# Joint decode in another order: three sparse key tiles of half 0 moved behind the forget-gate exponentials and between the first values

## What is computed

```python
def fox_attend(q, qpos, cq, segs):
    logits = concat([einsum('bthd,bshd->bhts', q, k) * ATTN_SCALE + cq_t - ck_t for k, _, _, ck in segs])
    pr = masked_softmax(logits, mask)          # exp(logits - max) / sum, over all past and new keys
    out = sum(einsum('bhts,bshd->bthd', pr_seg, v) for each segment)

def nsa_cmp_sel(q, qpos, ck_raw, cv_raw, sk, sv, p):
    ...                                         # compressed scores choose 16 blocks of 64 rows
    lg = einsum('bqgrd,bgqksd->bgrqks', q_c, kg) * ATTN_SCALE - slope * dist
    o = einsum('bgrqn,bgqnd->bqgrd', masked_softmax(lg, mask), vg)

def sample_layer(x, cache, page_table, p):
    o_cmp, o_sel = nsa_cmp_sel(qa, qpos, cat(c_cmp_k, ck), cat(c_cmp_v, cv), cat(c_sel_k, sk), cat(c_sel_v, sv), p)
    o_win = window_attend(...)
    o_fox = fox_attend(fq, qpos, c_new, ((past k, v), (new k, v)))
    h = merge_branches(x, o_cmp, o_sel, o_win, ng, o_fox, ga, gb, p)
```

## Time and profile before

| | us |
|---|---|
| median of 3 runs | 931.16 |
| lowest, highest | 929.49, 931.47 |
| the profiled execution's own time | 930.13 |
| its span | 927.4 |

### The profile page before, as it was taken

One profiled execution on the slowest core, in us unless ns is written; L12 is line 12 of the kernel. 1 busy time (PEld: TensorE's weight loads), 2 busy tenths in 40 slices (PEclk: granted clock), 3 DMA queues, 4 the chain that ended last, 5 costly groups with the idle time before them and its releaser, 6 DMA issues. The chain is left out here.

```text
span 927.4 us, 18075 instructions
## 1 busy us (share of the span) xinstructions
PE 859.7 (93%) x7225; PEld 704.6 (76%) x7225; DVE 518.3 (56%) x949; ACT 374.0 (40%) x694; POOL 160.6 (17%) x262
## 2 busy tenths in 40 slices
PE   2999888799999999999999977999979999999996
PEld 1888768689889977655755456997678988989884
DVE  5466568533434667654467434656665655656555
ACT  3346575642424323453224412445144434444330
POOL 1200041311121122333434510000010100101000
PEclk9999989999999999999999989999979999999999
DMA  5543096175424379989999994975064444554412
GB/s 168 189 158 119 5 313 240 64 160 144 153 93 183 102 314 371 335 312 421 415 416 418 379 404 140 289 244 171 1 225 138 137 136 157 198 188 136 136 45 61
DMA packets 90609, 191.89 MB, mean 207 GB/s; under 512 B 7434, under 2 KB 68651, under 8 KB 78155
## 3 DMA queue, kind: packets, MB, share of 16 engines
q0 software_dynamic: 15408, 106.04, 29.6%
q1 hardware_dynamic: 73836, 84.43, 29.4%
q10 hardware_dynamic: 1296, 0.45, 0.2%
HBM read 187.44 MB, written 7.64 MB: 210 GB/s over the span
## 5 line engine op out<-in xcount | busy, mean ns | idle before, releaser
L1604 PEld LDWEIGHTS banks<-consts_base,stream_rows 128*128 128x128 f32 x672 | 73.2, 141 | 30.9 <-issue 28.1
L1851 ACT ACTIVATE keys_turned<-banks 128x512 f32<-128x512 f32 x94 | 54.9, 596 | 100.3 <-PE banks L1604 100.2
L258 PE MATMUL banks<-tokens_turned_high,w_gates_high 128*128 128x288 f32 x288 | 86.6, 301 | 3.9 <-PEq L191 2.4
L1604 PE MATMUL banks<-consts_base,stream_rows 128*128 128x128 f32 x672 | 82.5, 276 | 4.7 <-PEq L191 1.7
L259 PE MATMUL banks<-tokens_turned_low,w_gates_high 128*128 128x288 f32 x288 | 85.2, 296 | 0.0
L1143 PE MATMUL banks<-chunks_turned_high,cmp_w_high 64*128 64x256 f32 (+1 forms) x512 | 76.7, 293 | 5.3 <-DVE cmp_w_low L251 2.7
L260 PE MATMUL banks<-tokens_turned_high,w_gates_low 128*128 128x288 f32 x272 | 81.6, 300 | 0.0
L1143 PE MATMUL banks<-chunks_turned_low,cmp_w_high 64*128 64x256 f32 (+1 forms) x512 | 73.6, 281 | 0.0
L1143 PE MATMUL banks<-chunks_turned_high,cmp_w_low 64*128 64x256 f32 (+1 forms) x512 | 73.4, 280 | 0.0
L1832 DVE COPY keys_turned<-banks 128x512 f32<-128x512 f32 x74 | 50.4, 689 | 29.6 <-PE banks L1604 27.1
L251 DVE TENSOR_TENSOR chunks_turned_low<-banks,chunks_turned_high 128x512 fp32r<-128x512 f32 x64 | 41.1, 683 | 44.4 <-ACT chunks_turned_high L246 44.4
(11 more groups left out here) (447 smaller groups left out, 2109.0 us busy)
## 6 DMA issues: line engine op xcount, KB each, us to landing
w_up_gate<-in_w_up SPq DMA_DIRECT2D x12, 1024.0 KB, 7.4
w_up_gate<-in_w_gate SPq DMA_DIRECT2D x12, 1024.0 KB, 9.9
w_down<-in_w_down SPq DMA_DIRECT2D x12, 1024.0 KB, 5.1
w_in_slot<-in_w_in SPq DMA_DIRECT2D x8, 1424.0 KB, 6.7
w_gates<-in_w_in SPq DMA_DIRECT2D x10, 512.0 KB, 7.6
cmp_w<-in_cmp_w_k SPq DMA_DIRECT2D x4, 512.0 KB, 8.5
cmp_w<-in_cmp_w_v SPq DMA_DIRECT2D x4, 512.0 KB, 11.6
stream_rows<-in_state_win_k SPq DMA_DIRECT2D x8, 256.0 KB, 8.5
```

The lines of the kernel that those rows point to most:

```text
L258: nc.tensor.matmul(out, lh, rh, start=start, stop=False, **kw)
L1604: ins = nc.tensor.transpose(bank(t)[:, q * P:(q + 1) * P], src, ident)
L1851: copy = lambda a, b: nc.scalar.activation(a, b, ACT.Copy)
```

## The change

The list is written in another order; no step is added, removed or altered. Before, `nsa(0, 1)` and `nsa(0, 2)` stood ahead of all exponentials of FoX half 0 and `nsa(0, 3)` and `nsa(0, 4)` among them. Now `nsa(0, 1)` stands behind exponentials 1 and 2, and `nsa(0, 2)` behind 3, 4 and 0. `nsa(0, 3)` and `nsa(0, 4)` go into `middle`, behind the second and the third value step. Behind them the key tiles `fox(1, 0)`, `fox(1, 1)` and `fox(1, 2)` come one value step later than before. From `fox(1, 3)` on the list is as it was.

```diff
@@ -1371,10 +1371,10 @@
-             + fox(0, 12) + select(0, 3) + fox(0, 13) + exps("win", 0, 0) + select(0, 4) + fox(0, 14) + select(0, 5) + fox(0, 15) + nsa(0, 1, 2)
-             + exps("fox", 0, 1, 2) + nsa(0, 3) + exps("fox", 0, 3, 4) + probs(0, 1) + exps("fox", 0, 0) + nsa(0, 4) + probs(0, 2))
-    middle = (vals(0, 0) + probs(0, 3, 4) + vals(0, 1) + probs(0, 0) + vals(0, 2) + fox(1, 0) + vals(0, 3) + exps("sel", 0, 0, 1) + fox(1, 1) + exps("sel", 0, 2, 3)
-              + vals(0, 4) + fold("fox", 0, 0) + fox(1, 2) + exps("sel", 0, 4) + vals(0, 5) + nsa_probs(0, 0, 1) + fox(1, 3) + vals(0, 6) + nsa_probs(0, 2, 3)
+             + fox(0, 12) + select(0, 3) + fox(0, 13) + exps("win", 0, 0) + select(0, 4) + fox(0, 14) + select(0, 5) + fox(0, 15)
+             + exps("fox", 0, 1, 2) + nsa(0, 1) + exps("fox", 0, 3, 4) + probs(0, 1) + exps("fox", 0, 0) + nsa(0, 2) + probs(0, 2))
+    middle = (vals(0, 0) + probs(0, 3, 4) + vals(0, 1) + nsa(0, 3) + probs(0, 0) + vals(0, 2) + nsa(0, 4) + vals(0, 3) + fox(1, 0) + exps("sel", 0, 0, 1) + vals(0, 4)
+              + fold("fox", 0, 0) + exps("sel", 0, 2, 3) + fox(1, 1) + vals(0, 5) + exps("sel", 0, 4) + fox(1, 2) + nsa_probs(0, 0, 1) + fox(1, 3) + vals(0, 6) + nsa_probs(0, 2, 3)
```

## The result

| | before | after |
|---|---|---|
| median, us (7 runs each, same chip) | 931.35 | 937.05 |
| lowest, highest | 929.49, 934.21 | 932.26, 941.28 |
| the profiled execution's own time, its span | 930.13, 927.4 | 941.28, 938.2 |

The changed kernel is slower: the ratio of the runs is 1.0056, with a 95% interval of 1.0034 to 1.0078, which is 3.2 to 7.3 us. The medians lie 5.7 us apart. The forecast was 936.6.

The account below looks back on a forecast made before the run. TensorE's order was taken to bound the decode stage early, DMA landings later. Stall 3.3, lost cover 0.5 and clock 2.5 make TensorE 6.3 us late; the end moves 5.4, 931.16 to 936.6 us, range 932.7 to 938.4.

Parts of the forecast that it names:

- What bounds the kernel: Decode stage: TensorE's order sets the pace from about 382 to 422 us, full DMA engines from 415 to 530.
- D: How much the stream of landings, and so the end, moves: 2.9 us, or 5.4 with the clock loss.
- P: TensorE's lateness where both orders meet, the turn of fox(1,3): 3.8 us, or 6.3 with the clock loss.
- Part 1, the stall: Behind the product of fox(0,15), TensorE waits for ScalarE's two exponentials and first key copy: 3.3 us lost, gap 3.2.
- Part 2, lost cover: Products of nsa(0,3) and fox(1,2) lose cover for their copies: 0.5 us in sum, bounds 0 and 0.9.
- Part 3, gathers and stream: Gathers after 394 us go out up to 5.4 us later; DMA idles about 2.5 us longer; landings move 2.9 us.
- Part 4, the clock: The gap near 395 us drops TensorE to 1.2 GHz for 6.8 us, costing 2.5 us, up to 3.4.
- The sum: The end of the kernel moves by D: 931.16 + 5.4 = 936.6 us.
- A: Rival: the stall at 395 us comes without a fall of the clock; 934.1 us, chance 0.37.
- C: Rival: the wait of 4.62 us at 538.14 absorbs the lateness; about 929 or 931 us, chance 0.08.
- E: Rival: the new order does nothing, a common wait behind it hiding it; chance 0.02.
- B: Rival: stall plus a longer low clock, or a second drop in the tail; 938 to 940 us, chance 0.06.

Follow-up runs that it names:

- e4: The kernel before with 28 unused transpositions (3.1 us of TensorE work) added ahead of the turn of nsa(0,2); 932.88 us, ratio 1.0029.
- e6: The kernel before with the same 28 unused transpositions ahead of half 1's turn of probabilities 0, near 505 us; 929.95 us, ratio 0.9996.
- e1: The changed kernel with nsa(0,1) and nsa(0,2) put back ahead of the exponentials; 931.22 us, ratio 1.0007.
- e2: The kernel before with only FoX exponentials 1 and 2 moved ahead of nsa(0,1) and nsa(0,2); 937.00 us, ratio 1.0057.
- e3: The changed kernel with 26 unused transpositions filling TensorE's gap ahead of the turn of probabilities 1; 933.74 us, ratio 1.0042.
- e7: The changed kernel with nsa(0,1) put back ahead of exponentials 1 and 2; 933.67 us, ratio 1.0032.
- e8: The changed kernel with exponential 1 alone ahead of nsa(0,1) and exponential 2 behind it; 932.70 us, ratio 1.0025.
- e5: The kernel before with GpSimd's two merge-weight loads issued five ring places later, behind the last selected values; 927.50 us, ratio 0.9978.

## Why the prediction was right

The time was 937.05 for a forecast of 936.6. Its steps, in their order:

- **What bounds the kernel.** Right, and shown by the pair e4 and e6: the same 3 us cost 2.0 us at 395 and at 505 nothing that can be measured. In all seven kernels with an early lateness D follows P, at a distance of 0.6 to 1.5 us, and the medians stand in nearly the order of D (and exactly in that of P): 0.4, 2.0, 2.5, 2.9, 3.5, 5.7 and 6.2 us over before for D of 0.22, 2.03, 2.98, 2.22, 3.52, 4.17 and 5.27.
- **Part 1, the stall.** Right in place, cause and size: a gap of 3.2 us was forecast, 3.12 came, released by the copy. TensorE goes on 4.18 us behind T0 (4.26 forecast), 3.2 us later than it would without the wait. e1 and e2 show that it is the exponentials' place and not the order of the ring.
- **Part 2, lost cover.** 0.5 us forecast. The rows show 0.67 before the product of fox(1,2) and 0.39 before that of nsa(0,3), where I had named both, less the 0.27 that goes: 0.8, inside the bounds of 0 to 0.9.
- **Part 3, gathers and stream.** The gathers at T0 + 8.6 and + 11.5 were forecast without the clock, T0 + 10.04 and + 12.82 came with it. D = P - 0.9 was forecast, P - 1.07 came. Each of the early kernels bears out that D falls somewhat short of P. The hole in the stream was forecast 2.5 us longer than before's without the clock; with it, the bytes missing over 40 us are worth 4.4 us. The page of the Trainium skill that I had set against it (DMA: Bandwidth & Descriptors, Where 436 GB/s comes from), with HBM binding at about 358 GB/s, is not what this core shows: 407 GB/s over 119 us in after, 411 before.
- **Part 4, the clock.** It fell, as forecast, and e3 shows that this matters for P. Its size is the term of the sum that was off: 2.5 us forecast, with bounds of 1.8 to 3.4, from a low stretch of 6.8 us, but here the low stretch lasted from about 401.6 to 405.1, 3.4 us, nearly all of it behind the gap, and cost (2.01 - 1.1) + (1.62 - 1.0) = 1.5 us. In e2 the low stretch was 6.8 us; of its P of 5.95 the stall is 3.3 (TensorE goes on at T0 + 4.28 instead of + 1.00), which leaves 2.7 for the clock, near the 2.5. So P came out as 5.24 in the profiled execution. By terms it is 3.2 + 1.5 + 0.8 = 5.5; 0.3 us less were measured, for which no cause is known.
- **The sum.** By the profiled execution D is 4.17 instead of 5.4, under the 4.5 that P = 5.6 and D = P - 1.1, the lower bounds, would have given, and the end moves by 4.6; the median moves by 5.7, with an interval that holds both. I can't say whether the other executions had the long low stretch or the short one, since only one was profiled. So the closeness of 936.6 to 937.05 is in part luck: the clock's term was too large for the execution that can be read.
- **The rivals.** A (no fall of the clock, 934.1) is what e3 comes to: P 3.71 for 3.8, D 2.22 for 2.9, 933.7 us. As a mechanism A held; it only wasn't this kernel, whose P of 5.24 lies halfway between A's 3.8 and the forecast's 6.3. C (absorbed) fails for the reason given, the dry stretch at 402; e6 is where C is true. E fell with the result. B came in part: the clock did fall again in the tail of after, where TensorE alone sets the pace, at 0.57 over 582 to 586 us, where before kept 1.00. TensorE, first after and then before:

```profile
582.60 0.58 PE L258 MATMUL banks<-branch_out_high,w_o_high 128*128 128x288 f32 x1 [2.82 <-DVE branch_out_low L251]
...
587.37 0.29 PE L258 MATMUL banks<-tokens_turned_high,w_gates_high_early 128*128 128x288 f32 x1
```

```profile
576.07 0.29 PE L258 MATMUL banks<-tokens_turned_high,w_gates_high_early 128*128 128x288 f32 x1
```

After needs 4.77 us between the two steps, before 3.27 (from 572.80), so this fall cost 1.5 us. It doesn't show as D + 1.5 at the end, because TensorE is only 3.6 us late at 582.60: behind the tile of D before still had the low clock of its own long wait (0.62 over 542 to 545), after no longer. With it the end moved by 4.6 us, and not by B's 7 to 9.

## What to carry to other kernels

An engine that copies out of PSUM for TensorE must not have an instruction that waits for a late result queued ahead of these copies: here two exponentials of 0.7 us, moved ahead of three copies, cost some 5 to 6 us (after and e2), since the copies waited with them for the maximum. Before a step is moved, ask in which of the stage's parts it lies: where the DMA queue is nearly empty, because the gathers wait for TensorE to free their slots, its lateness goes into the end less 0.6 to 1.5 us, and where the DMA queue is full 3 us of it cost nothing that was measured, and there the order of the bytes is what pays (two weight loads moved behind the last urgent tiles gave 2 to 2.7 us).

## What the runs showed of the hardware that I had not expected

**A fall of the clock is not decided by the gap ahead of it.** It fell after gaps of 2.03 us (e7), 3.12 (after) and 3.21 (e2), and stayed after 2.42 (e8). At one and the same step (L258) and behind the same gap of 2.82 us it stayed in before (572.80) and fell in after (582.60). And in after it fell at about 302.7 us with TensorE busy all through the stretch ahead (4.00 of 4.00 us at 296 to 300 in the second row of the first fence, and no wait from 290 on), at a place where the profiled execution of before kept 1.00. At 183.83 it fell in after behind a gap of 2.80 us, where before had a gap of 2.71 and kept it. The other profiled executions show either, with no edit there. What decides it stays open.

**How long it stays low differs too**: 3.4 us in after and e7, 6.8 in e2, at the same place of nearly the same program, and 10.2 us in before from about 114 us on.

**The rate of the full DMA engines depends on what they carry.** At a busy share of 1.01 to 1.03 it was 422 GB/s in e5 at 529 to 533 us, where before had 325, and 331 in e5 at 541 to 546, where the merge weights had moved to. That it is the weights is read from the times of their landings and from the low rate moving with them.

**So one execution's time says little here.** Two stretches of 6.8 us at the lower clock, which can cost 3.4 us each, account for the 6.17 us that the profiled execution of after lost ahead of the change, more than the whole change in the median. Only distances from a common step within the trace, and medians of many runs, could be compared at all.
